# Weights split once: their high and low parts kept in DRAM scratch by the first block of tokens

## The reference

```python
h = modulate(rms_norm(x, norm1_g), shift1, scale1)
proj = h @ w_in           # attention q, k, v; deltanet q, k, v, beta, decay; out gate; two branch gates
o_attn = sliding_window_attention(q, k, v, sinks)
o_dn = gated_delta_rule(...)            # chunked, with a state carried from chunk to chunk
merged = sigmoid(gate_a) * (o_attn @ w_branch[:512]) + sigmoid(gate_d) * (o_dn @ w_branch[512:])
x = x + gate1 * (merged @ w_out)
h = modulate(rms_norm(x, norm2_g), shift2, scale2)
x = x + gate2 * ((silu(h @ w_gate) * (h @ w_up)) @ w_down)      # hidden width 2816
```

## Time and profile before

| | |
|---|---|
| median of 3 runs | 3195.29 us (3195.13 to 3199.54) |
| the profiled execution | 3193.09 us, its span 3191.4 us |
| busy: TensorE | 3052.6 us, 96% |
| busy: VectorE, ScalarE, GpSimd | 1649.5, 1215.8 and 89.9 us |
| instructions | 39552 |
| DMA, mean over the span | 112 GB/s |
| loads of weight units | 492 of 512 KB, 3.5 us median from issue to landing |

### The profile page before, as it was taken

How to read it: one execution, slowest core, us unless ns; L and a number is a source line. 1 busy time by engine, 2 the same in 40 slices (tenths; PEclk the granted TensorE clock), 3 DMA queues, 4 the chain that set the end, 5 groups by cost and what they waited for, 6 DMA issues and landing times.

```text
span 3191.4 us, 39552 instructions
## 1 busy us (share of the span) xinstructions
PE 3052.6 (96%) x15696; PEld 2565.9 (80%) x15696; DVE 1649.5 (52%) x2656; ACT 1215.8 (38%) x1969; POOL 89.9 (3%) x84
## 2 busy tenths in 40 slices
PE   3999998999999999999999999999999999999999
PEld 3897787888888777888889777788888977878887
DVE  6777475443466645434355755543436575543333
ACT  2545433232255543323235544332323554432222
POOL 0000000000000000000000000000000000000000
PEclk9999998999999999999999999999999999999999
DMA  6343253332433323323243342333334342323233
GB/s 255 108 157 111 73 181 140 104 97 95 133 105 110 109 83 132 101 97 98 94 132 111 98 123 76 127 103 96 99 98 132 119 116 88 105 93 94 97 99 99
DMA packets 136856, 358.19 MB, mean 112 GB/s; under 512 B 38112, under 2 KB 38240, under 8 KB 135008
## 3 DMA queue, kind: packets, MB, share of 16 engines
q1 hardware_dynamic: 132320, 347.27, 33.7%
q10 hardware_dynamic: 4352, 8.39, 0.7%
HBM read 326.25 MB, written 29.36 MB: 111 GB/s over the span
## 4 chain that ended last, share of the span: by engine, by line
PE 83%; DVE 5%; issue 4%; ACT 2%; DMA 2%; SPq 1%; DVEq 1%; POOL 0%; POOLq 0%; ACTq 0%
PE gb L1542 63%; PE gb L1559 7%; PE gb L1845 4%; PE mb L1717 3%; PE mb L1689 1%; DVE tmp_c L1275 1%; DVE inv_c L1278 1%; DVE w_lo L1000 1%; DMA lc_u<-scratch_u 1%; PE mb L1631 1%; PE mb L1712 1%; DMA w_raw<-in_wstream 0%; PE mb L1764 0%; PE mb L1765 0%; PE mb L1699 0%
## 5 line engine op out<-in xcount | busy, mean ns | idle before, releaser
L1542 PE MATMUL gb<-h_hi,w_hi 128*128 128x512 f32 x2336 | 928.3, 397 | 27.3 <-DVE h_lo L1023 19.5
L632 ACT ACTIVATE w_hi<-w_raw 128x1024 fp32r<-128x1024 f32 x492 | 518.5, 1057 | 1081.4 <-PE gb L1542 967.7
L1542 PE MATMUL gb<-h_lo,w_hi 128*128 128x512 f32 x2336 | 924.1, 396 | 0.0
L1542 PE MATMUL gb<-h_hi,w_lo 128*128 128x512 f32 x2336 | 923.0, 395 | 0.0
L1000 DVE TENSOR_TENSOR w_lo<-w_raw,w_hi 128x1024 fp32r<-128x1024 f32 x492 | 600.2, 1222 | 508.2 <-ACT w_hi L632 507.3
L1542 PEld LDWEIGHTS gb<-h_hi,w_hi 128*128 128x128 f32 x2336 | 445.1, 191 | 123.1 <-issue 12.9
L1542 PEld LDWEIGHTS gb<-h_hi,w_lo 128*128 128x128 f32 x2336 | 445.3, 191 | 93.9 <-issue 1.5
L1542 PEld LDWEIGHTS gb<-h_lo,w_hi 128*128 128x128 f32 x2336 | 445.5, 191 | 92.7 <-issue 1.5
L1542 PE MATMUL gb<-hid_hi,w_hi 128*128 128x512 f32 x704 | 274.0, 389 | 0.0
L1542 PE MATMUL gb<-hid_hi,w_lo 128*128 128x512 f32 x704 | 273.9, 389 | 0.0
L1542 PE MATMUL gb<-hid_lo,w_hi 128*128 128x512 f32 x704 | 273.9, 389 | 0.0
(11 more groups left out here) (268 smaller groups left out, 3506.6 us busy)
## 6 DMA issues: line engine op xcount, KB each, us to landing
w_raw<-in_wstream SPq DMA_DIRECT2D x492, 512.0 KB, 3.5
ada_buf<-in_ada_w SPq DMA_DIRECT2D x11, 2048.0 KB, 8.9
x<-in_x SPq DMA_DIRECT2D x4, 2048.0 KB, 9.4
out<-x ACTq DMA_DIRECT2D x16, 512.0 KB, 3.5
xs<-in_x SPq DMA_DIRECT2D x12, 512.0 KB, 4.6
scratch_nt<-st_nt SPq DMA_DIRECT2D x16, 256.0 KB, 2.5
scratch_at<-st_at SPq DMA_DIRECT2D x16, 256.0 KB, 2.9
scratch_kd<-st_kd SPq DMA_DIRECT2D x16, 256.0 KB, 3.1
```

The costliest lines, as they stand in the source:

```text
L632: act.activation(w_hi[s][:, :], w_raw[s][:, :], ACT.Copy).then_inc(w_high.sem, 1)
L1542: last = pe.matmul(bank(j), w, r, start=(i == 0), stop=(i == n - 1))
```

## The change

Block 0 works as before, and after each split also stores both parts of the unit, now side by side in one buffer, to DRAM scratch: 1024 KB a unit (`keep_unit`). In blocks 1 to 3 neither ScalarE nor VectorE splits; SP loads both parts of unit u in one transfer of 1024 KB, once TensorE has used unit u-3, and TensorE waits for the landing instead of the split. In block 0, ScalarE also waits for the store of unit u-3 before it overwrites that slot. Since loads in blocks 1 to 3 are issued later than in block 0 with respect to TensorE's work, the other transfers in SP's loop are tied to `ahead`, which is u + 2 there.

```diff
-    w_hi = [sb(f"w_hi{s}", [P, UW], fp32r) for s in range(RING)]
-    w_lo = [sb(f"w_lo{s}", [P, UW], fp32r) for s in range(RING)]
+    w_pair = [sb(f"w_pair{s}", [P, 2, UW], fp32r) for s in range(RING)]
+    w_hi, w_lo = [[w_pair[s][:, i, :] for s in range(RING)] for i in range(2)]
...
+    kept = nc.dram_tensor("scratch_w", (U_PER, P, 2, UW), fp32, kind="Internal").ap()
...
+    w_kept = [sig(f"w_kept{s}", 16 * U_PER // RING) for s in range(RING)]
...
+    def wait_used(eng, b, u):
+
+        which, n = LAST_USE[u % U_PER]
+        signal = full if which == "full" else half_done
+        eng.wait_ge(signal.sem, signal.at(b, n + u // U_PER * signal.per))
...
             def load_unit(b, u):
-                sp.wait_ge(w_ready.sem, b * U_PER + (u + 1))
-                sp.dma_start(w_raw[u % RING][:, :], wstream[u]).then_inc(w_loaded[u % RING].sem, 16)
+                s = u % RING
+                if b:
+                    if b == 1 and u < RING:
+                        keep_unit(U_PER - RING + u)
+                        sp.wait_ge(w_kept[s].sem, w_kept[s].at(1, 0))
+                    wait_used(sp, b, u - RING)
+                    sp.dma_start(w_pair[s][:, :, :].bitcast(fp32), kept[u]).then_inc(w_loaded[s].sem, 16)
+                    return
+                if u >= RING:
+                    keep_unit(u - RING)
+                sp.dma_start(w_raw[s][:, :], wstream[u]).then_inc(w_loaded[s].sem, 16)
+
+            def keep_unit(u):
+
+                sp.wait_ge(w_ready.sem, w_ready.at(0, u + 1))
+                sp.dma_start(kept[u], w_pair[u % RING][:, :, :].bitcast(fp32)).then_inc(w_kept[u % RING].sem, 16)
...
                 for u in range(U_PER):
-                    if u in (U_Z + 2, U_GATE, U_GATE + 2, U_GATE + 4):
-                        park(b, (u - U_Z - 2) // 2)
-                    if u == U_GATE + 4:
+                    ahead = u + 2 if b else u
+                    if ahead in (U_Z + 2, U_GATE, U_GATE + 2, U_GATE + 4):
+                        park(b, (ahead - U_Z - 2) // 2)
+                    if ahead == U_GATE + 4:
                         gather(b)
...
             def split(b, u):
                 s = u % RING
-                if b * U_PER + u >= NB * U_PER:
+                if b * U_PER + u >= U_PER:
                     return
-                act.wait_ge(w_loaded[s].sem, b * w_loaded[s].per + 16 * (u // RING + 1))
-                unit_used(b, u - RING)
+                act.wait_ge(w_loaded[s].sem, 16 * (u // RING + 1))
+                if u >= RING:
+                    wait_used(act, 0, u - RING)
+                    act.wait_ge(w_kept[s].sem, 16 * (u // RING))
                 act.activation(w_hi[s][:, :], w_raw[s][:, :], ACT.Copy).then_inc(w_high.sem, 1)
...
+            def wait_weights(b, u):
+
+                if b:
+                    pe.wait_ge(w_loaded[u % RING].sem, w_loaded[u % RING].at(b, 16 * (u // RING + 1)))
+                else:
+                    pe.wait_ge(w_ready.sem, w_ready.at(0, u + 1))
```

More of the change, by code:

```diff
@@ L512, in _ @@
                 for u in range(U_PER):
-                    if u in (U_Z + 2, U_GATE, U_GATE + 2, U_GATE + 4):
-                        park(b, (u - U_Z - 2) // 2)
-                    if u == U_GATE + 4:
+                    ahead = u + 2 if b else u
+                    if ahead in (U_Z + 2, U_GATE, U_GATE + 2, U_GATE + 4):
+                        park(b, (ahead - U_Z - 2) // 2)
+                    if ahead == U_GATE + 4:
                         gather(b)
-                    if u == U_GATE + 11:
+                    if ahead == U_GATE + 11:
                         write_images(b)
-                    if u == U_GATE + 12:
+                    if ahead == U_GATE + 12:
                         sp.wait_ge(imaged.sem, imaged.at(b, 32 * NBASE))
@@ L525, in _ @@
                         load_triangles(1)
-                    if u in (U_BRANCH - 1, U_BRANCH + 1, U_BRANCH + 3):
-                        done = (u - U_BRANCH + 1) // 2
+                    if ahead in (U_BRANCH - 1, U_BRANCH + 1, U_BRANCH + 3):
+                        done = (ahead - U_BRANCH + 1) // 2
                         sp.wait_ge(z_prod.sem, z_prod.at(b, done + 1))
@@ L533, in _ @@
                         load_products(done + 1)
-                    if u == U_OUT + 5:
+                    if ahead == U_OUT + 5:
                         sp.wait_ge(full.sem, full.at(b, J_OUT))
@@ L996, in split @@
                 s = u % RING
-                if b * U_PER + u >= NB * U_PER:
+                if b * U_PER + u >= U_PER:
                     return
-                dve.wait_ge(w_high.sem, b * U_PER + (u + 1))
+                dve.wait_ge(w_high.sem, u + 1)
                 dve.tensor_tensor(w_lo[s][:, :], w_raw[s][:, :], w_hi[s][:, :].bitcast(fp32), ALU.subtract
@@ L1535, in by_feature @@
                 if first == 0:
-                    pe.wait_ge(w_ready.sem, w_ready.at(b, u + 1))
+                    wait_weights(b, u)
                     free_bank(b, j)
```

## The result

The changed kernel takes 3207.04 us (median of 8 runs, 3204.18 to 3209.21) against 3195.7 for the kernel before: ratio 1.0034, 95% interval 1.0023 to 1.0044. It is slower by 11 us, inside the predicted range and 6 above the predicted time. The profiled span is 3206.8 us; its steps are compared with the span of before, 3191.4. These two single executions differ by 15.4 us, 4 more than the medians.

A forecast was written before the change was run, and what follows sets the result against it. TensorE, busy 96% of the span, was taken as the bound. Terms -6.0 + 1.0 + 3.0 + 0 + 6.0 + 2.1 = +6.1 us, added to the median of 3195.29, gave 3201 us; range 3187 to 3217.

The forecast's parts named there:

- rival 1: Whole kernel: small net of gains and costs, as summed, 3190 to 3204 us; chance 0.45.
- rival 2: Block 0's feed-forward stretch: bound by its DMAs, up to 16 us more, 3201 to 3217; chance 0.28.
- Gate stage, 2.0 us a block: Blocks 1 to 3: removing splits shortens softmax and deltanet-output chains, gaining 2.0 us a block, 6.0 in three.
- rival 4: Gate stages, blocks 1 to 3: freed engines shorten gaps, less low clock, 7 us a block more gained; chance 0.22.
- Triangles, 1.0 us a block: Blocks 1 to 3: deltanet triangle loads follow a 1024 KB load, costing 1.0 us a block (bounds 0 and 2.9).
- Block 0's gate stage, 6.0 us: Triangles and values there each stand behind an added store, costing 3.0 us each (bounds 0 and 7.2 together).
- Block 0's feed-forward stretch, 0 us: 68 added stores fit the DMA rate at 3.0 us per 1024 KB, costing nothing (bounds 0 and 16).
- The ring takes up the bunching: Block 0's feed-forward stretch: the ring of unit slots absorbs bunched transfers, costing nothing.
- Seam, 2.1 us: Between blocks 0 and 1: last stores and first loads queue in SP's order, costing 2.1 us once (0.5 to 4.3).
- The price of a DMA: All added transfers: 1024 KB takes 3.0 us of transfer (2.5 to 3.6), 5.0 us from issue to landing.
- Rival 3: Blocks 1 to 3: single loads land late behind interleaved pairs, 8.5 us a block, 25 in all, 3226; chance 0.05.
- Single loads, 0.3 a block: Last group of down units, blocks 1 to 3: one load 0.3 us late a block, 1.0 in three.

The follow-up runs named there:

- e8: Changed kernel with triangles ahead of their unit load in every block, `ada_w` part 10 behind `xs`, block 0's last values one unit earlier: 3184.7 us.
- e10: Kernel before with the three moves of e8, the last values one unit earlier in every block: 6.7 us less than the kernel before.
- e1: Changed kernel with the stores of units 120 to 122 ahead of block 1's first load: 3207.19 us.
- e11: Changed kernel with, in block 0 alone, triangles ahead of unit 31's store and load and the last values one unit earlier: 3201.36 us.
- e3: Changed kernel with part 10 of `ada_w` (2048 KB) moved from unit 61 to 63, behind the last `xs` part: 3201.07 us.
- e7: Kernel before with part 10 of `ada_w` two units later, behind the feed-forward's `xs`: 3.9 us less than the kernel before.
- e2: Changed kernel with the triangles of blocks 1 to 3 ahead of unit 32's load: 3197.65 us.
- e6: e8 with the stores of units 120 to 122 also ahead of block 1's first load: 1.1 us from e8.
- e12: e8 without the stores behind unit 2, so blocks 1 to 3 load wrong weights: 3173.85 us.

## Why the prediction was right, and where it was not

The stated range and the sign of the sum (+6.1) hold; measured is +11.3. That it came so near is in good part luck. The result lies 3 us above the band of rival 1, the small net (3190 to 3204), and in that of rival 2 (3201 to 3217), whose mechanism did not come; and of the terms some were off by as much as the result and cancelled: the gate stages gave 11 us more than summed, and the triangles, block 0's feed-forward stretch and the seam took 5 to 6, 9 and 3 more.

- *Gate stage, 2.0 us a block: mis-sized.* It is worth 5.7 (17.0 in three, splits given back), and where no triangle is late 6.1 against the kernel before (traces of e8 and before) or 5.8 against the same order (e8 and e10). The step that failed is "0.2 us" and "for the other two I take 0.3" for the deltanet outputs: the wait for `t_o` fell by 2.3 us a block. I took GpSimd's power as a fixed producer that "ends only at 1154.32"; but its 1.92 us were that long only with a split beside it, and without one it takes 1.01. The softmax gave less than the 1.5 a block that I had: its waits fell from 6.0, 6.3 and 6.0 us to 4.9, 5.3 and 5.0. Between the traces of before and e8, waits make up 2.7, 4.8 and 3.2 us of the 6.0, 6.0 and 6.4 that the three blocks gained, and TensorE's own pace the rest. So rival 4 had the direction. Its reason, the clock by shorter gaps, is not shown, since block 2 had the high clock before with the longer waits; its size, 7 us a block beside the 2.0, was too large.
- *Triangles, 1.0 us a block: mis-sized.* TensorE's waits for them in blocks 1 to 3 rose from 1.6 us to 9.0, 2.5 a block, and moving them was worth 9.4 us, 3.1 a block in the median (2.8 by the ratios, 4.6 in the traces): about my upper bound of 2.9. I set the ScalarE copy without its split and the quieter engines against the load ahead. What I left out is that a faster gate stage needs its triangles earlier: from the start of unit 29 to that of unit 30, just ahead of them, the kernel after won 2.2, 1.4 and 2.0 us in the three blocks, and by unit 31 it had lost 4.9, 2.1 and 2.2. So with the gain the slack was mis-sized too, as far as these starts show. The load from issue to landing took 8.51 us.
- *Block 0's gate stage, 6.0 us: right.* 5.7 in the two traces (up to 8 by e1's), and 5.7 back by e11.
- *Block 0's feed-forward stretch, 0 us: wrong*, 9.1 measured, within the bounds of 0 and 16. The sign named for rival 2, a wait for a split in that stretch, came; but rival 2 had the place right, not the mechanism. The rate sufficed: the same bytes pass in e3, in another order, and the time does not come back later. "The ring takes up the bunching" failed because a split does not only wait for its weight: it stands in ScalarE's queue behind the norm of an `xs` part, and this behind 2048 KB in SP's. This link stood in the trace before as 7.51 us, and TensorE already waited 1.7 us behind it: had I read that wait of the earlier trace rows back to it, the term would not have been 0. (The other wait there, 6.1 us, is not behind `xs`, though what was expected of e7 says so: it lies in the first 100 us, and e7's trace still has it, 6.9 us.) e3 took 6 us of the term away with one number.
- *Seam, 2.1 us: mis-sized*, 4.9 measured. I counted the stores and loads of SP's queue. ScalarE writes `out` there too, four transfers of 512 KB, and the store took 9.06 us to land where mine took 8.0, the load behind it 6.96 where mine took 5.0. That these writes are the reason is not shown, since no run takes them away; e1 shows that the order of the stores is not.
- *The price of a DMA: right to the landing.* 1024 KB land in 4.8 us as a load and 5.0 as a store; I had 5.0. In the seam, two such loads issued 0.36 us apart (884.44 and 884.80) land 2.48 us apart (889.21 and 891.69): there the transfer costs the cheap end, 2.5, where I took 3.0. Rival 3 did not come: no unit behind an interleaved pair waits for its load. The Trainium skill, "DMA: Bandwidth & Descriptors", Bandwidth, has 6.15 us for 1 MB in a load issued by GpSimd; the loads here are issued by SP and land in 4.8 us, so this trace differs.
- *Single loads, 0.3 a block: right*, 0.3 to 0.4 at unit 118 (5.0 less 4.76 is 0.24, which I had rounded up). *Other transfers tied to `ahead`: nothing*, right in blocks 1 to 3.

Still open: why TensorE's busy time in the gate stage fell by 1.0 to 3.3 us and its clock is 0.99 in every gate stage of blocks 1 to 3 once splits and late triangles are gone (e2, e6, e8, e12), and whether the change with its order mended is worth its 4.3 us against the kernel before with the same moves.

## What to carry to other kernels

Traffic that fits the rate is not free: in this kernel it cost where a small transfer with a tight date stands behind large ones with none. Before adding a transfer per step, list for each queue what has the least slack and what will stand ahead of it, other engines' writes included, and move those first; here three moves in the order of issue were worth 22 us, twice the loss, and 7 us even to the kernel that had none of the traffic. A wait named after one engine (a split) is to be followed to the first thing late in its chain, and work taken off two engines that feed each other is to be costed over the whole stage, not at the last link. Before a producer is taken as fixed, look at the same instruction elsewhere in the trace: here GpSimd's power had two durations, 1.92 and 1.01 us, and the longer one went with the work that was to be removed.

## What was not expected of the hardware

- GpSimd's power of 128x4 elements takes 1.92 us when VectorE splits a weight unit at the same time and 1.01 us when it does not: 12 and 4 times in the kernel before, 3 and 13 times in the kernel after.
- In the kernel before the same loss shows now as clock, now as waits: the gate stage of block 1 has 129.64 us of matmuls at a granted clock of 0.96 and 9.3 us of waits, that of block 2 127.38 at 0.99 and 11.6 of waits, and they take 139.1 and 139.3 us. Where the clock was higher, TensorE waited longer for the others, and the stage was no shorter.
- A raw load of 512 KB behind a store takes 6.1 us to land instead of 3.5, and 2048 KB 11.6 instead of 8.9: each 2.6 or 2.7 us more, about the 2.5 us by which 1024 KB put the next landing off in the seam.
